# Weights' halves placed 16 bytes later, and the activations that stream over them at one distance modulo 256

## What is computed

```
h = rms_norm(x, gain)                        # second block: then * (1 + scale) + shift
x = x + 0.5 * (silu(h @ w_gate) * (h @ w_up)) @ w_down     # 8 times; inner width 2,816
x = x + mixer(rms_norm(x, gain))             # 4 times
```

## Time and profile before

| | |
|---|---|
| median of 3 runs | 2831.4 us (2829.68 to 2831.49) |
| profiled execution, its own time | 2825.14 us |
| its span, first to last instruction | 2823.4 us |
| PE busy | 2742.8 us, 97% |
| VectorE busy | 2130.7 us, 75% |
| ScalarE busy | 1567.9 us, 56% |
| DMA, share of 16 engines | 49.4%, 507 MB |

### The profile page before, as it was taken

One profiled execution on the slowest core, in us unless ns is written; L12 is line 12 of the kernel. 1 busy time (PEld: TensorE's weight loads), 2 busy tenths in 40 slices (PEclk: granted clock), 3 DMA queues, 4 the chain that ended last, 5 costly groups with the idle time before them and its releaser, 6 DMA issues.

```text
span 2823.4 us, 61154 instructions
## 1 busy us (share of the span) xinstructions
PE 2742.8 (97%) x26372; PEld 2622.2 (93%) x26372; DVE 2130.7 (75%) x3179; ACT 1567.9 (56%) x2377; POOL 14.0 (0%) x23
## 2 busy tenths in 40 slices
PE   7999999999999999999999999999999999998999
PEld 7999878899999998788999999888999989998999
DVE  7878667688888787666788798667878876777864
ACT  6545644456555455544465565476656646676653
POOL 0000000000000000000000000000000000000000
PEclk9999999999999999999999999899999999999999
DMA  6674311246756753111556567433775764432453
GB/s 232 253 285 180 135 42 44 84 165 239 264 209 248 284 206 130 66 47 47 179 209 250 216 241 271 177 120 130 259 268 209 260 242 165 149 135 105 165 191 138
DMA packets 72941, 511.12 MB, mean 181 GB/s; under 512 B 8480, under 2 KB 9248, under 8 KB 11872
## 3 DMA queue, kind: packets, MB, share of 16 engines
q1 hardware_dynamic: 72672, 507.22, 49.4%
HBM read 506.13 MB, written 1.05 MB: 180 GB/s over the span
## 4 chain that ended last, share of the span: by engine, by line
PE 83%; DVE 10%; ACT 4%; issue 2%; DMA 1%; SPq 0%; DVEq 0%; ACTq 0%
PE solve_banks L2043 13%; PE solve_banks L2045 13%; PE solve_banks L2044 13%; PE linear_banks L2037 4%; PE linear_banks L2043 4%; PE linear_banks L2045 4%; PE linear_banks L2044 4%; PE linear_banks L2038 4%; PE linear_banks L2039 3%; DVE split_halves L1347 3%; PE linear_banks L2606 3%; PE linear_banks L2607 3%; PE linear_banks L2608 3%; PE solve_banks L2468 1%; PE linear_banks L2434 1%
## 5 line engine op out<-in xcount | busy, mean ns | idle before, releaser
L1347 DVE TENSOR_TENSOR split_halves<-raw_units,split_halves 128x1024 fp32r<-128x1024 f32 x806 | 972.6, 1221 | 315.2 <-ACT split_halves L933 313.1
L933 ACT ACTIVATE split_halves<-raw_units 128x1024 fp32r<-128x1024 f32 x806 | 840.4, 1053 | 439.9 <-PE solve_banks L2045 199.0
L2043 PE MATMUL solve_banks<-h_split,split_halves 128*128 128x256 f32 x1792 | 498.4, 278 | 3.3 <-DVE split_halves L1347 3.1
L2045 PE MATMUL solve_banks<-h_split,split_halves 128*128 128x256 f32 x1792 | 498.1, 278 | 0.0
L2044 PE MATMUL solve_banks<-h_split,split_halves 128*128 128x256 f32 x1792 | 497.5, 278 | 0.0
L2043 PE MATMUL solve_banks<-hidden_split,split_halves 128*128 128x256 f32 x1408 | 396.0, 281 | 0.0
L2045 PE MATMUL solve_banks<-hidden_split,split_halves 128*128 128x256 f32 x1408 | 395.7, 281 | 0.0
L2044 PE MATMUL solve_banks<-hidden_split,split_halves 128*128 128x256 f32 x1408 | 395.7, 281 | 0.0
L2043 PEld LDWEIGHTS solve_banks<-h_split,split_halves 128*128 128x128 f32 x1792 | 335.9, 187 | 4.8 <-DVE split_halves L1347 2.4
L2045 PEld LDWEIGHTS solve_banks<-h_split,split_halves 128*128 128x128 f32 x1792 | 336.4, 188 | 0.0
L2044 PEld LDWEIGHTS solve_banks<-h_split,split_halves 128*128 128x128 f32 x1792 | 336.4, 188 | 0.0
(11 more groups left out here) (341 smaller groups left out, 5851.0 us busy)
## 6 DMA issues: line engine op xcount, KB each, us to landing
raw_units<-in_stream SPq DMA_DIRECT2D x403, 1024.0 KB, 4.8
raw_units<-in_mod_w SPq DMA_DIRECT2D x72, 1024.0 KB, 6.2
x<-in_x SPq DMA_DIRECT2D x4, 256.0 KB, 4.6
w2a<-in_w2a SPq DMA_DIRECT2D x2, 512.0 KB, 6.2
w_rows<-in_w SPq DMA_DIRECT2D x2, 512.0 KB, 7.6
bs_rows<-in_bs SPq DMA_DIRECT2D x2, 512.0 KB, 8.4
spatial_t<-in_ws_t SPq DMA_DIRECT2D x2, 512.0 KB, 9.9
out<-x SPq DMA_DIRECT2D x4, 256.0 KB, 4.2
```

The costliest lines, as they stand in the source:

```text
L933: nc.scalar.activation(split[:, n % SPLIT_SLOTS, 0, :], raw[:, item % RAW_SLOTS, (n % 2) * HALF * P:(n % 2 + 1) * HALF * P], ACT.Copy).the ...
L1347: V.tensor_tensor(split[:, n % SPLIT_SLOTS, 1, :], raw[:, item % RAW_SLOTS, (n % 2) * HALF * P:(n % 2 + 1) * HALF * P], split[:, n % SPLIT ...
L2043: M(bank[:, 0:T], w_hi, a[:, 0, :], start=start, stop=False, skip_group_check=True)
L2045: return M(bank[:, 0:T], w_lo, a[:, 0, :], start=False, stop=stop, skip_group_check=True)
```

## The change

The diff puts `split_halves` 4 floats (16 bytes) into a tensor of its own room, so that its tiles lie at 144 modulo 256. `modulation` moves from ahead of `x` to behind `h_split`. With that, `h_split`, `hidden_split`, the mixers' outputs and `rough_split` all begin at 160, 16 bytes behind the weights modulo 256. The rows of `rough_split` are 320 columns apart (1,280 bytes, five times 256), so all of them are at 160 too. For the norms 8 and 11, those ahead of the two attentions, where `h_split` is the stationary operand, `h_of` puts it 12 floats later, at 208, which is 64 from the weights as before; for L2089 to L2091 the distance becomes 16. Small tensors (`silu`, `final_rstd`, `unit_biases`, sums) get other places in the arena, and most other tensors lie 96 bytes later than before. The instructions of every engine, their order, their sizes and their waits are the same as before, row for row; only addresses differ.

```diff
+SPLIT_AT = 4
+ROOM = 12
+ARENA_PAD = 0
+H_AT = {n: 12 if n in (8, 11) else 0 for n in range(13)}
+ROUGH_ROW = 320
...
-    split = place("split_halves", [P, SPLIT_SLOTS, 2, HALF * P], F32R)
+    split_room = place("split_halves", [P, SPLIT_AT + SPLIT_SLOTS * 2 * HALF * P], F32R)
+    split = split_room[:, SPLIT_AT:].rearrange("p (s a t) -> p s a t", s=SPLIT_SLOTS, a=2)
+    x = place("x", [P, DT, T])
+    h_room = place("h_split", [P, 2 * DT * T + ROOM], F32R)
     mod = place("modulation", [P, 144])
-    x = place("x", [P, DT, T])
-    h = place("h_split", [P, DT, 2, T], F32R)[:].rearrange("p c a t -> p a c t")
...
-    arena = at[0] + (-at[0]) % 32
+    arena = at[0] + ARENA_PAD
...
-    silu = over("silu", [P, 3, T], 62)
+    silu = over("silu", [P, 3, T], 101)
...
-    final_rstd = over("final_rstd", [P, T], 60.75)
-    rough = over("rough_split", [P, 2, DT, T + 2], 44.25, F32R)
+    final_rstd = over("final_rstd", [P, T], 78)
+    rough = over("rough_split", [P, 2, DT, ROUGH_ROW], 44, F32R)
...
-    unit_bias = over("unit_biases", [P, 3, 2], 60.5)
+    unit_bias = over("unit_biases", [P, 3, 2], 64.25)
...
+    def h_of(n):
+
+        a = H_AT[n]
+        return h_room[:, a:a + 2 * DT * T].rearrange("p (c a t) -> p a c t", c=DT, a=2)
...
-        o = h[:, part, c, :]
+        o = h_of(n)[:, part, c, :]
...
-                pair_tiles(w, unit_banks(i, j), ready)
+                pair_tiles(w, unit_banks(i, j), h_of(ffn_norm(i)), ready)
...
-                    a_hi, a_lo = (h[:, a, c, j * CH:(j + 1) * CH] for a in range(2))
+                    a_hi, a_lo = (h_of(8 + 3 * key[1])[:, a, c, j * CH:(j + 1) * CH] for a in range(2))
```

More of the change, by code:

```diff
@@ L464, in build_program @@
     kkn = over("key_norms", [HEADS, T], 72)
-    va_sum = over("va_sums", [P, NCH, 4], 104.25)
-    va_stat = over("va_stats", [P, 4, NCH], 104.3125)
-    ln_b1024 = over("ln_b_1024", [P, DT], 104.375)
+    va_sum = over("va_sums", [P, NCH, 4], 104.125)
+    va_stat = over("va_stats", [P, 4, NCH], 104.15625)
+    ln_b1024 = over("ln_b_1024", [P, DT], 104.1875)
     u_ = over("u", [P, DT, T], 56)
@@ L1020, in split_h @@
                     if n < 6:
-                        nc.scalar.activation(h[:, 0, c:c + len(tiles), :],
+                        nc.scalar.activation(h_of(n)[:, 0, c:c + len(tiles), :],
                                              pieces[:, c // 2 % 2, c % 2:c % 2 + len(tiles), :], ACT.Copy)\
@@ L1174, in rwkv @@
                     act.wait_ge(merged_ready, 4 * l + s + 1)
-                    nc.scalar.activation(h[:, 0, 2 * s:2 * s + 2, :], merged[:, 2 * s:2 * s + 2, :], ACT.Copy)\
+                    nc.scalar.activation(h_of(3 * l + 1)[:, 0, 2 * s:2 * s + 2, :], merged[:, 2 * s:2 * s + 2, :], ACT.Copy)\
                         .then_inc(merged_hi, 1)
@@ L1420, in norm @@
                     if n < 6:
-                        V.tensor_tensor(h[:, 1, c:c + len(tiles), :],
+                        V.tensor_tensor(h_of(n)[:, 1, c:c + len(tiles), :],
                                         pieces[:, c // 2 % 2, c % 2:c % 2 + len(tiles), :],
-                                        h[:, 0, c:c + len(tiles), :].bitcast(F32), ALU.subtract).then_inc(h_ready, 1)
+                                        h_of(n)[:, 0, c:c + len(tiles), :].bitcast(F32), ALU.subtract)\
+                            .then_inc(h_ready, 1)
                     else:
@@ L1708, in merged_rest @@
                 dve.wait_ge(merged_hi, 4 * l + s + 1)
+                h = h_of(3 * l + 1)
                 V.tensor_tensor(h[:, 1, w, :], merged[:, w, :], h[:, 0, w, :].bitcast(F32), ALU.subtract)\
@@ L2073, in two_tiles, with halves_of_h @@
                 ins.then_inc(lin_filled, 1)
-            HH = (h[:, 0, :, :], h[:, 1, :, :])
+            def halves_of_h(l):
+                h = h_of(3 * l + 1)
+                return h[:, 0, :, :], h[:, 1, :, :]
             def tokens_major(w, key, width):
                 bank = bank_for(key)
+                h = h_of(3 * key[1] + 1)
                 for i in range(2):
@@ L2140, in unit_tiles, with pair_tiles @@
                 unit_free(i, j)
-                pair_tiles(w, unit_banks(i, j), ready)
-            def pair_tiles(w, banks, ready=None):
+                pair_tiles(w, unit_banks(i, j), h_of(ffn_norm(i)), ready)
+            def pair_tiles(w, banks, h, ready=None):
                 order = [(e, k) for k in range(DT) for e in range(2)] if ready else \
@@ L2239, in rwkv @@
                     else:
-                        two_tiles(base + 2 * s, ("shift", l, s), (HH, HH),
+                        two_tiles(base + 2 * s, ("shift", l, s), (halves_of_h(l),) * 2,
                                   h_wait(3 * l + 1) if s == EARLY_UNITS else None)
@@ L2281, in rwkv @@
                 for s in range(4):
-                    two_tiles(base + 2 * (17 + s), ("u", l, s), (HH, HH))
+                    two_tiles(base + 2 * (17 + s), ("u", l, s), (halves_of_h(l),) * 2)
                     if s == 1:
@@ L2315, in rwkv @@
                     if b and i in GATE_STEPS:
-                        part_products(("gate", l, c + 1), gates + 2 * (c + 1), HH, i, GATE_STEPS)
+                        part_products(("gate", l, c + 1), gates + 2 * (c + 1), halves_of_h(l), i, GATE_STEPS)
                     if c == DT - 1:
@@ L2347, in rwkv @@
                         wait_emptied(pe, ("out", l, d - 2))
-                    pair_tiles(OUT_AT[l] + 2 * d, wide_banks(("out", l, d)),
+                    pair_tiles(OUT_AT[l] + 2 * d, wide_banks(("out", l, d)), h_of(3 * l + 1),
                                (lambda k: pe.wait_ge(merged_split, 4 * l + k // 2 + 1)) if d == 0 else None)
```

## The result

The kernel after takes 2850.09 us in the median of four runs (2847.5 to 2851.46), the one before 2830.54 (2825.3 to 2831.49): a ratio of 1.0072, 95% interval 1.0054 to 1.0089. It is slower by some 20 us, where 52 us less was forecast and the range ended at 2840. The rival "the slow pace everywhere" had said 2853; it is near by its number, though no settled stretch of the kernel after runs at its 117.8 ns. The profiled execution took 2849.16 us, span 2847.4.

What follows compares the result with a forecast made beforehand. The prediction took TensorE, busy 97% of the span, as the bound, through each matmul's cost above its columns. Five terms summed to 51.9 us, from 2831.4 to 2779.5 us, range 2710 to 2840.

Steps and rivals of the forecast that it cites:

- the slow pace everywhere: Rival for all moving-activation matmuls: +16 settles at 117.8 ns in every stretch, 2853 us; chance 0.14.
- The reading of the two paces: TensorE's weight and column reads obstruct each other, depending on distance modulo 256 and falling into step: 113.3 or 117.8 ns.
- the price at +16: Matmul pace at the new distance: unknown, bounded by 106.7 and 119 ns, taken as 113.3 ns.
- 1, gate-and-up: Four slow gate-and-up stretches of 960 matmuls gain 4.44 ns each: 17.1 us saved.
- 2, down stretches: Eight down stretches, 4,224 matmuls over `hidden_split`, gain 4.44 ns each: 18.8 us saved.
- 3, mixing stages: `h_split` in the mixing stages: about 1,800 of 2,592 matmuls are slow and speed up, 8.0 us saved.
- 4, mixers' outputs: Matmuls over the mixers' outputs: half of 1,150 are slow and speed up, 2.5 us saved.
- 5, rough tiles: 960 rough-tile matmuls go from about 119 ns to 113.3: 5.5 us saved.
- the reversed matmuls: 2,736 matmuls kept out: distance stays 64 at the attentions; 384 of L2089 to L2091 could change 1.7 us at most.
- the zero for VectorE and ScalarE: New operand addresses on the other engines were costed at nothing; mean durations of L1347 and L933 stay.
- Units arrive in time: In gate-and-up and down stretches VectorE and DMA keep up with faster TensorE, so nothing is taken off the gain.
- the likeliest case: Every moving-activation matmul runs at 113.3 ns: 2779.5 us, own range 2768 to 2795; chance 0.42.

Runs made afterwards that it cites:

- e3: Kernel after, but weights back at 128, `h_split` at 144 (distance 16), `hidden_split`, mixers' outputs and rough tiles at 128 (distance 0); 2844.47 us.
- e4: Kernel after, but weights at 128 and each gate-and-up stretch at its own distance, 0 to 160 bytes; 2857.62 us.
- e9: Kernel after, but weights at 128 and moving activations at distance 112, except first block's mixer outputs and attention norms; 2794.5 us, ratio 0.9851 to the kernel before.
- e1: Kernel before, unchanged, profiled a second time; 2829.26 us, against 2835.72 for the kernel before beside it.
- e12: Kernel after, unchanged, profiled a second time; 2863.67 us.
- e6: Kernel after, but weights at 160, `h_split` at 176 (distance 16), `hidden_split` and the others at 192 (distance 32); 2834.62 us.
- e8: Kernel after, but weights at 128, `h_split` and `hidden_split` at 144 (distance 16), mixers' outputs at 128, rough tiles at 160; 2845.87 us.
- e7: Kernel after, but weights at 128 and a second sweep of distances by norm, with three gate-and-up stretches at 112; 2843.8 us.
- e11: As the run at distance 112 from weights at 128, but two small tables ahead of `x`, putting `h_split` 368 bytes from weights modulo 512; 2794.26 us.

## Why the prediction was wrong

**The reading of the two paces** held in part. That both run with no wait and a full clock all windows show, and that addresses have to do with it e3, e4 and e9 do. That how a stretch is entered decides between them fits the changes at interruptions (e1), but what it is in the entry no run shows. By the Trainium skill's rule (SBUF — State Buffer, section "SBUF: two separate sides"), that TensorE never waits on anyone at its ports, no distance would have mattered. The measurement decides otherwise: in e4, with the same instructions, 120.0 ns at distance 96 and 113.3 at 112. That the two reads meet in the memory is still only argued; no record shows such a stall. How busy DMA is makes no difference: the last window of e1 has 885 matmuls at a DMA share of 0.54, others 885 at 0.68. Whether the writes of VectorE and ScalarE into `split_halves` have a part, no run separates.

**The step that failed is the price at +16**, "I take 113.3 ns". Its reason was that "a distance which is the same for all operands should leave no place where streams are pushed out of step". A common distance does not select the better pace; each distance has a set of its own, and 16 from weights at 144 has 117.3 and 120.0 (the kernel after and e12, 16 stretches, 118.5 on average). The rough tiles, which I named as the bound from above (119 ns) and set aside, were the only rows that visited +16 at all. And I chose the value nearest to what the code could do at +64, which says nothing about +16.

**A second miss was the weights' place.** I treated the change as one of distance and did not ask what 16 bytes do to the weights alone. In e3 distance 16 with weights at 128 had 113.3 in three stretches; moving both by 16 took that pace away (profiles of after and e12: none in 16 stretches). Leaving the weights at 128 would not have saved the forecast: at distance 16 only 5 of the 24 stretches of e3, e6 and e8 ran at 113.3.

The terms, forecast against profiled: 1, gate-and-up, -17.1 us, came as +16.2. 2, down stretches, -18.8, came as nearly 0: their mean went from 117.78 to 117.75 ns. 3, mixing stages, -8.0, came as +3. 4, mixers' outputs, -2.5, came as +3. 5, rough tiles, -5.5, came as -2. That the reversed matmuls stay at 113.3 where their distance stays 64 held (a window of 13 us in the dilated attention has 117, as against 118 in the earlier trace rows), and so did the zero for VectorE and ScalarE. "Units arrive in time" held in e9, where the faster pace was there: 1.5% less time, with DMA at 0.76 to 0.82 in all down stretches but the last.

The forecast of the likeliest case as such, all at 113.3, 2779.5, is 15 us under what e9 took, which has that pace in all gate-and-up and down stretches: 2794.5. The mixers' outputs of the first block were at distance 96 there, on a chip where the kernel before took 2836.4.

## What to carry to other kernels

When a kernel's float32r matmuls follow each other without a gap and still stand further apart than their columns take, count them in windows and look at the addresses of both operands modulo 256. A distance has to be measured, not reasoned, and with enough stretches to see all of its paces: one profile shows a draw. Of all that was tried here, weights at a multiple of 32 with moving operands 112 bytes on, modulo 256, were the one choice with the single pace of 113.3 ns (35 gate-and-up and down stretches of e7, e9 and e11), worth 1.5% of the whole kernel.

## What was not expected of the hardware

At one set of addresses TensorE has up to three stable paces (113.3, 116.7 and 118.7 ns for 256 columns at distance 16), holds one for as long as matmuls follow without a pause, and hands it to the next stretch where the distance is the same (e8). No distance went below 113.3 ns, 6.7 over the columns' 106.7.

The surcharge is there at the full clock only. At the granted clock of 0.50 the 18 rough tiles from 1004.47 to 1008.09 us stand 213.35 ns apart, and 256 columns at 1.2 GHz are 213.3. In the kernel before, at distance 64, 13 matmuls at that clock (from 324.3 us on) stand 213.3 ns apart too. In this execution of the kernel after, the clock was at that level after 3.04 us without work, which cost some 2 us more.
